# One knob of an attention stage: both heads' transposes back to back, the whole turn's projection steps behind them

## The reference

```python
xn = rms_norm(x, norm_mix_w)
proj = xn @ w_in                                  # columns: b, c, h (conv) | q, k, v, 512 each
yc = b * causal_depthwise_conv3(c * h)            # then RMS norm per group of 64 channels
# stick-breaking attention, 8 heads of 64, queries in blocks of 128, strictly causal
z = (rms_norm(q) @ rms_norm(k).T) / sqrt(64)
suffix = cumsum of log_sigmoid(-z) from the right, shifted by one key
A = where(mask, exp(log_sigmoid(z) + suffix), 0)
ya = A @ v                                        # then RMS norm per head
x = x + concat([yc, ya]) @ w_out
x = x + moe(rms_norm(x))                          # top 1 of 4 groups, then top 2 of 8 experts
```

## Time and profile before

| | before |
|---|---|
| device time, median of 3 runs | 1246.56 us (1245.02 to 1247.19) |
| the profiled execution's own time | 1245.32 us |
| its span | 1243.6 us |
| TensorE matmul busy | 1114.1 us (90%) |
| VectorE busy | 876.5 us (70%) |
| ScalarE busy | 723.9 us (58%) |

### The profile page before, as it was taken

One profiled execution on the slowest core, in us unless ns is written; L12 is line 12 of the kernel. 1 busy time (PEld: TensorE's weight loads), 2 busy tenths in 40 slices (PEclk: granted clock), 3 DMA queues, 4 the chain that ended last, 5 costly groups with the idle time before them and its releaser, 6 DMA issues. The chain is left out here.

```text
span 1243.6 us, 16698 instructions
## 1 busy us (share of the span) xinstructions
PE 1114.1 (90%) x5806; PEld 909.2 (73%) x5806; DVE 876.5 (70%) x918; ACT 723.9 (58%) x890; POOL 143.0 (12%) x193
## 2 busy tenths in 40 slices
PE   5998999999999869993589999999999999999920
PEld 4886777778778548883378888888888888888810
DVE  4405657576574563225579999999999999999816
ACT  4422655746633532111378888888888888888800
POOL 1001000000000310000101111111111111111000
PEclk9999999999999979995599999999999999999965
DMA  6111010110011362006279999999999999999219
GB/s 205 55 34 35 18 34 18 34 35 19 23 34 30 136 248 90 35 34 280 100 279 371 373 392 393 377 380 389 387 381 379 387 385 381 384 382 387 96 35 387
DMA packets 57338, 261.88 MB, mean 211 GB/s; under 512 B 13008, under 2 KB 33488, under 8 KB 43984
## 3 DMA queue, kind: packets, MB, share of 16 engines
q1 hardware_dynamic: 46928, 240.31, 50.7%
q0 software_dynamic: 9216, 16.80, 3.6%
q10 hardware_dynamic: 1152, 4.19, 0.8%
HBM read 252.88 MB, written 25.17 MB: 224 GB/s over the span
## 5 line engine op out<-in xcount | busy, mean ns | idle before, releaser
L1265 DVE TENSOR_TENSOR e_lo<-W,e_hi 128x1024 fp32r<-128x1024 f32 x384 | 452.6, 1221 | 25.8 <-ACT e_hi L1259 23.0
L1259 ACT ACTIVATE e_hi<-W 128x1024 fp32r<-128x1024 f32 x384 | 403.3, 1060 | 97.0 <-PE ps L1230 97.0
L1228 PE MATMUL ps<-e_hi,xT_hi 128*128 128x512 f32 x512 | 204.4, 399 | 7.1 <-DVE e_lo L1265 7.1
L1230 PE MATMUL ps<-e_lo,xT_hi 128*128 128x512 f32 x512 | 201.6, 394 | 0.0
L1229 PE MATMUL ps<-e_hi,xT_lo 128*128 128x512 f32 x512 | 201.0, 393 | 0.0
L744 DVE TENSOR_TENSOR_SCAN kept<-kept,start_at 128x1024 f32<-128x1024 f32 (+7 forms) x64 | 91.2, 1425 | 65.3 <-ACT kept L597 65.3
L417 PE MATMUL ps<-xnT_hi,w_hi 128*128 128x512 f32 x320 | 128.4, 401 | 2.4 <-DVE y_mix L719 0.9
L417 PE MATMUL ps<-xnT_hi,w_lo 128*128 128x512 f32 x320 | 128.1, 400 | 0.0
L417 PE MATMUL ps<-xnT_lo,w_hi 128*128 128x512 f32 x320 | 125.0, 391 | 0.0
L606 ACT ACTIVATE probsT<-ps 128x512 f32<-128x512 f32 (+3 forms) x96 | 43.8, 491 | 128.9 <-PE ps L466 128.8
L1228 PEld LDWEIGHTS ps<-e_hi,xT_hi 128*128 128x128 f32 x512 | 97.6, 191 | 27.0 <-issue 4.0
(11 more groups left out here) (211 smaller groups left out, 1670.6 us busy)
## 6 DMA issues: line engine op xcount, KB each, us to landing
W<-in_w_dram SPq DMA_DIRECT2D x96, 2048.0 KB, 10.3
w_raw<-in_w_in_dram SPq DMA_DIRECT2D x20, 512.0 KB, 4.0
yy<-y_rows SPq DMA_DIRECT2D x8, 1024.0 KB, 13.5
xt<-in_x_dram SPq DMA_DIRECT2D x8, 512.0 KB, 3.7
w_out_raw<-in_w_out_dram SPq DMA_DIRECT2D x4, 1024.0 KB, 8.0
xn_rows<-xn SPq DMA_DIRECT2D x8, 512.0 KB, 2.6
out_dram<-x ACTq DMA_DIRECT2D x8, 512.0 KB, 8.9
x<-in_x_dram SPq DMA_DIRECT2D x1, 3072.0 KB, 14.9
```

Of the source, the lines that this page charges most:

```text
L1228: pe.matmul(o, xs_hi[:, k], e_hi[:, p, cols], start=(k == 0), stop=False)
L1230: mm = pe.matmul(o, xs_hi[:, k], e_lo[:, p, cols], start=False, stop=(k == last))
L1259: act.activation(e_hi[:, p], flat[:, p * D:(p + 1) * D], ACT.Copy).then_inc(s["hi_made"], 1)
L1265: dve.tensor_tensor(e_lo[:, p], flat[:, p * D:(p + 1) * D], e_hi[:, p], ALU.subtract).then_inc(s["lo_made"], 1)
```

## The change

Two constants. In the first three pairs the 24 ticks of a turn all come behind the transposes of head 1, and none between the heads; in the last pair, where two groups are made in each of the turns r = 0 to 3, both groups (48 ticks) come behind the transposes of head 1. Every engine's instructions stay the same ones. VectorE's `take` of the last pair moves with it: `groups_in(n, 0)` is empty, and `groups_in(n - 1, 1)` has two groups.

```diff
-SHARE = ((8, 16),) * 8
-SHARE_LAST = ((24, 24),) * 4 + ((0, 0),) * 4
+SHARE = ((0, 24),) * 8
+SHARE_LAST = ((0, 48),) * 4 + ((0, 0),) * 4
```

## The result

The changed kernel takes 1274.45 us (median of 6 runs, 1271.21 to 1277.17) against 1246.6: 1.0224 times the time of before, 95% interval 1.0207 to 1.0241. The forecast was 1270.3 in a range of 1262 to 1277. The profiled execution has a span of 1273.1 us, 29.5 more than before. The six runs of the changed kernel lie 6 us apart and the six of before 3 us, but that is no effect of the change: the 17 runs of the kernel before that were made beside e8 and e9 lie 6.2 us apart (1242.6 to 1248.8).

The account below looks back on a forecast made before the run. In the first three pairs TensorE's issue plus small waits bound the time. First three pairs +9.3, last pair +10.8, clock +3.6 give +23.7 on 1245.3: 1269.0 profiled, 1270.3 us as median (1.2 higher), range 1262 to 1277.

Parts of the forecast that it names:

- a low granted clock in turns with short pauses: Sign in the profile after that would show the forecast wrong, the clock falling beyond the two long idle stretches.
- the share of the clock: TensorE restarting at half clock behind two long idle stretches, turns 0 and 24: 1.8 us each, +3.6 us.
- rival D: Clock also falls at five shorter pauses (turns 25, 26, three turns with sums), 1.8 us each: 1279 us; chance 10%.
- The transpose banks, r = 1 to 3: First three pairs: head 1's transposes wait for ScalarE's copies out of both full banks; +2.0 us a pair.
- Turns 8 and 16: Turns r = 0: the bank wait and the wait for VectorE's read of bank 7 overlap; -0.36 us each.
- Turns r = 5 to 7: One half to a row, banks free: only the saved switch between matmuls and transposes, about -0.2 us a pair.
- Turn 0: VectorE still late for head 1, eight ticks go behind it: +1.8 us, 3.0 us idle, plus 1.8 us clock.
- The last pair: Turns 24 to 27: group B waits for VectorE's delayed read of group A; +10.8 us, turn 24 alone +5.4.
- Rival C: Last pair: VectorE's queue no hindrance, one 0.8 us read per joint, 4.6 for 10.8 us; 1262 us; chance 6%.
- The turns with the sums: Turn r = 4 of three pairs: eight ticks no longer cover the wait for ScalarE's chain; +0.94 us each.
- Rivals A and B: A: order is free, 1246 to 1248 us, chance 2%. B: faster as head 1 comes earlier, 1241, chance 2%.
- E: Clock falls at every bank wait, about sixteen turns at 1.8 us: 1297 us; chance 2%.

Follow-up runs that it names:

- e8: Kernel before, with no ticks between heads only in turns 8, 16, r = 5 to 7, and eight ticks between head 1 and the sums in turns 4, 12, 20; 1242.37 us.
- e9: As e8, with the last group of all moved from behind head 1 of turn 27 to turn 28; 1239.13 us (0.9955).
- e5: Changed kernel, but 3 of the 24 ticks stay between the heads in turns r = 1 to 3 of the first three pairs; 1266.42 us.
- e4: Changed kernel, but in the three turns with the sums (r = 4) the ticks are (8, 16) as before; 1270.31 us.
- e6: Changed kernel with four matmuls of no use in the pause ahead of the sums of the keys in turns 4, 12 and 20; 1271.39 us.
- e3: Changed kernel, but in the last pair VectorE reads group A between its two weighs instead of behind both; 1269.13 us.
- e2: Kernel before with only the last pair's half of the change, (0, 48) ticks in turns 24 to 27; 1260.58 us (1.012).

## Why the prediction was right

The time lies in the range, and every wait that was priced is there. But the prediction named a sign of being wrong, a low granted clock in turns with short pauses, and that sign came: the share of the clock is mis-sized, 11.0 us in place of 3.6, and what the forecast has as rival D is in large part what happened.

- *The transpose banks, r = 1 to 3.* Forecast 2.0 us for a pair, measured 2.1 to 2.2. Head 1 started at 1.44 us where 1.34 was worked out: what follows the end of the copy is 0.15 us and not the 0.05 taken for a semaphore. Right in mechanism (e5), short by that tenth.
- *Turns 8 and 16.* Forecast -0.36, measured -0.36 and -0.35. Turns r = 5 to 7: forecast -0.2, measured -0.11 to -0.26.
- *Turn 0.* Forecast 1.8 and 1.8 of clock, measured 3.54, in e4 and e5 4.2 and 4.1.
- *The last pair.* Forecast 10.8 and 1.8 of clock; the four turns grew by 7.06, 4.09, 1.54 and 1.42, 14.1 in all, of which 1.7 and 1.6 are clock in turns 24 and 25 (half of the 3.4 us that B ran at 0.50; turn 25 without the fall is the 18.50 of e6). The fall in turn 24 was forecast, the one in turn 25 not. That leaves 10.8. VectorE's queue ahead of the read is the cause (e3). Rival C, one exposed read at each joint, is refuted by e2, and with it the sum that "Perfetto Trace Analysis", Optimizing Tensor Performance, Matmuls, in the Trainium skill would have given: its rule on rotating banks names the place, but not the price.
- *The turns with the sums.* The step that failed is the last one of this part: "+0.94, in each of three pairs", with no lost clock. The 0.94 itself was exact (0.95 in e6), but 3.0 + 1.35 + 1.35 of clock come on top. Rival D had named these pauses and turn 25's at a chance of 10%, with the argument against them that a pause of 2.7 us had kept its clock. That argument doesn't hold. The row ends with the pause and shows nothing of the clock behind it, and the execution was a lucky one: behind the same pause the clock fell in the nine other profiles that have it. Of D's five pauses four lost the clock, at 3.0, 1.3, 1.3 and 1.6 us where 1.8 each was priced; the one in turn 26 didn't.
- *The sum.* Attention ends 31.6 us later: 20.6 without clock, where 20.1 was forecast, and 11.0 of clock, where 3.6 was. Of these 11.0, the places that were forecast have 3.4 (turns 0 and 24), the turns with the sums 5.65, turn 25 1.6 and turn 29 0.4. So attention is 7.9 us over its forecast, and the median only 4.2 over: there is luck in that. Some 2 us came back behind attention in this execution (791.8 us from there to the end against 793.9), but that stretch took 791.6 to 794.9 in the ten profiles other than e9's, whose code is the same there, so this is scatter and no effect. And the 1.2 us by which the median lay above the profiled execution before had no counterpart after (the profiled one took 1274.77). Rivals A and B are out: nothing ran faster but turns 8, 16 and r = 5 to 7, together 1.3 us. E is out too: the clock never fell at the waits of 0.3 to 0.7 us for the transpose banks, fifteen of them (sixteen at 1.8 us are 28.8, so E's own sum is 1299 and not 1297).

## What to carry to other kernels

Filler work between two dependent pieces covers different waits in different turns, so a uniform rule for where it goes is worth less than one read off each turn: ask for each place what the next instruction waits for without it, and how many tenths of a microsecond that takes (here 3 ticks did for what 8 were spent). Where two groups share a bank, what counts is not the read but all that stands ahead of it in the reader's queue. And price a new pause on TensorE with the clock that it may cost: a pause of 1 us lost up to 3 us more. Don't judge that from one execution: the one pause by which it was judged here kept its clock in one profile of ten.

## What the runs showed of the hardware

- Behind transposes, sixteen matmuls of two columns and a pause of 1.03 us the granted clock fell from 2.4 to 1.2 GHz in 9 of 12 turns. With four matmuls of no use (0.9 us) in the pause it stayed up in all three turns (e6): work without a purpose made the turns shorter.
- The longer pauses of turns 1 to 29, and those of the joints and banks, gave over the eleven profiles: 5.7 to 5.8 us in turn 24, a fall in 6 of 6; 2.65 us in turn 29, in 9 of 10; 1.83 us behind a full group in turn 25, in 5 of 6 (all but e6); 1.55 (turn 24 of e3), 1.37 (turn 26 of e6) and 1.20 us (turn 28 of e9), in none; 0.8 to 0.9 us at the joints and 0.3 to 0.7 us at the transpose banks, in none. So the length of a pause alone doesn't tell: 1.03 us behind the small sums lost the clock in 9 of 12 turns, 1.37 and 1.55 us right behind a full group in neither of two. That it is the small sums which make the difference is argued and was not tested by itself.
- "TensorE: Matmul & The Clock Gate", section Why this matters for your kernels, in the Trainium skill advises to keep idle gaps out from between bursts of matmuls, as the clock falls in them. It speaks of longer gaps than most of these. The trace agrees for the pause of 5.7 us, and goes beyond the advice: the clock also fell behind 1.03 us, in 9 of 12 turns.
- Such falls come in some executions and not in others: turn 4, with the same instructions on TensorE, takes between 13.1 and 16.1 us from profile to profile. The spread of the times doesn't show it, as the kernel before has one as wide. The mean granted clock of the whole run does show the loss in every run: 0.936 to 0.940 in the six of the changed kernel, 0.944 to 0.949 in those of the kernel before.
